# Adding the squares of the feed-forward norms on VectorE instead of GpSimd in a two-layer decoder trunk

## What is computed

```python
def rms_norm(x, g):
    xf = x.astype(jnp.float32)
    y = xf * lax.rsqrt(jnp.mean(xf * xf, axis=-1, keepdims=True) + EPS)
    return y.astype(x.dtype) * g

for l in range(DEPTH):                       # DEPTH = 2
    if l == 0: xp = xp + attention_a(rms_norm(xp, g_attn[0])) @ w_o_a[0]
    else:
        k, v = rms_norm(xp, g_kv) @ w_kv_s   # shared keys and values
        xp = xp + attention_b(rms_norm(xp, g_attn[1]), k, v) @ w_o_b[0]
    gate, up = rms_norm(xp, g_ffn[l]) @ w_gate_up[l]
    xp = xp + (silu(gate) * up) @ w_down[l]
y = rms_norm(xp, g_final)
```

## Time and profile before

| | |
|---|---|
| median of three runs | 2483.86 us (2478.34 to 2485.71) |
| the profiled execution | 2487.55 us, of which the span is 2485.8 |
| PE busy | 2366.3 us, 95% of the span |
| DVE, ACT, POOL busy | 1588.7, 812.5, 265.8 us |
| mean granted clock of PE | 0.976 of full speed |

### The profile page before, as it was taken

One profiled execution on the slowest core, in us unless ns is written; L12 is line 12 of the kernel. 1 busy time (PEld: TensorE's weight loads), 2 busy tenths in 40 slices (PEclk: granted clock), 3 DMA queues, 4 the chain that ended last, 5 costly groups with the idle time before them and its releaser, 6 DMA issues. The chain is left out here.

```text
span 2485.8 us, 43568 instructions
## 1 busy us (share of the span) xinstructions
PE 2366.3 (95%) x17709; PEld 2277.6 (92%) x17709; DVE 1588.7 (64%) x3174; ACT 812.5 (33%) x1863; POOL 265.8 (11%) x216
## 2 busy tenths in 40 slices
PE   8999899999999999998999998787999999999996
PEld 8888699999999999998999876477999999999996
DVE  6466647776766767667212377557767667676666
ACT  4344435222222222224110187544222222222224
POOL 3343200000000000004211110521000000000002
PEclk9999999999999999999999999888999999999998
DMA  4010211141313131110221233711131313131112
GB/s 179 21 54 18 90 51 40 47 150 48 114 49 113 52 110 43 52 48 21 87 70 42 83 95 135 266 51 35 52 112 50 113 49 119 44 110 52 51 35 73
DMA packets 79043, 187.93 MB, mean 76 GB/s; under 512 B 10968, under 2 KB 40024, under 8 KB 78072
## 3 DMA queue, kind: packets, MB, share of 16 engines
q1 hardware_dynamic: 77944, 180.45, 22.3%
q0 software_dynamic: 912, 4.85, 0.5%
HBM read 175.85 MB, written 44.70 MB: 89 GB/s over the span
## 5 line engine op out<-in xcount | busy, mean ns | idle before, releaser
L1532 DVE TENSOR_TENSOR XT<-XT,PS 128x768 f32<-128x768 f32 x382 | 257.9, 716 | 112.4 <-PE PS L2474 111.2
L2474 PE MATMUL PS<-HH,SLH 128*128 128x384 f32 (+1 forms) x1050 | 231.8, 329 | 8.1 <-DVE XT L1532 6.0
L2474 PE MATMUL PS<-HL,SLH 128*128 128x384 f32 (+1 forms) x1050 | 231.2, 328 | 0.0
L2474 PE MATMUL PS<-HH,SLL 128*128 128x384 f32 (+1 forms) x1050 | 231.0, 328 | 0.0
L2377 PE MATMUL PS<-TH_T,SLH 128*128 128x272 f32 x1056 | 219.0, 289 | 2.4 <-issue 2.4
L2377 PE MATMUL PS<-TL_T,SLH 128*128 128x272 f32 x1056 | 219.6, 289 | 0.0
L2377 PE MATMUL PS<-TH_T,SLL 128*128 128x272 f32 x1056 | 219.4, 289 | 0.0
L2474 PEld LDWEIGHTS PS<-HH,SLH 128*128 128x128 f32 x1050 | 177.4, 188 | 9.9 <-issue 9.9
L2474 PEld LDWEIGHTS PS<-HL,SLH 128*128 128x128 f32 x1050 | 178.1, 188 | 0.0
L2474 PEld LDWEIGHTS PS<-HH,SLL 128*128 128x128 f32 x1050 | 178.0, 188 | 0.0
L2377 PE MATMUL PS<-TH_B,SLH 128*128 128x272 f32 x792 | 166.6, 292 | 6.2 <-DVE SLL L1579 6.2
(11 more groups left out here) (323 smaller groups left out, 5303.9 us busy)
## 6 DMA issues: line engine op xcount, KB each, us to landing
ROW<-in_w_gu SPq DMA_DIRECT2D x88, 512.0 KB, 3.6
ROW<-in_w_dn SPq DMA_DIRECT2D x44, 512.0 KB, 4.0
out_bkS<-in_bk_in SPq DMA_DIRECT2D x8, 2032.0 KB
out_bvS<-in_bv_in SPq DMA_DIRECT2D x8, 2032.0 KB
KC<-in_bk_in SPq DMA_DIRECT2D x8, 1536.0 KB, 10.5
VC<-in_bv_in SPq DMA_DIRECT2D x8, 1536.0 KB, 7.0
XT<-in_xT SPq DMA_DIRECT2D x16, 544.0 KB, 5.4
RAW<-in_w_qB SPq DMA_DIRECT2D x12, 512.0 KB, 3.6
```

The source lines that it names most:

```text
L1532: ins = nc.vector.tensor_tensor(x, x, ps, ALU.add)
L2474: ins = mm(PS[:, 3 * j + i, 0:width], w[:, k * P:(k + 1) * P], x[:, a:a + width], start=(k == 0 and n == 0), stop=(k == 1 and n == 2))
```

## The change

It has three parts. All squares of norms 2, 3 and 4 are added on DVE, and POOL adds none. For norms 2 and 4, the squares of the eight tiles get a place each (tile 0's is the total itself), so ACT does not wait for adds and tile 0 needs none; norm 2's adds stand together behind the loop, norm 4's stand in it. In the second output projection, ACT squares a tile after the operands and not ahead of them, DVE adds the square of the tile before, `T1`'s low parts come one tile later and `T2`'s after tile 5, with the piece lists changed to match.

```diff
 PIECES_LO = (
...
-    ["B110", "B111", "B112", "B210", "T10", "T20", "T30", "B211", "T11", "T21", "T31", "B212", "T12", "T32", "T22", "D6",
-     "D7", "B220", "B221", "B222", "T42", "T40", "T41"])
+    ["B110", "B111", "B112", "B210", "T30", "B211", "T31", "T10", "B212", "T32", "T11", "D6", "T20", "T21", "D7", "T22", "T12",
+     "B220", "B221", "B222", "T42", "T40", "T41"])
...
-        SQ2, SQS2 = at("SQ2", [P, 2, TOK], R), at("SQS2", [P, MT * P], R + 2 * W4)
-        SQ_OF, SQS_OF = (SQ, SQ1, SQ2, SQ1, SQ2), (SQS, SQS1, SQS2, SQS1, SQS2)
+        SQS2 = at("SQS2", [P, MT * P], R)
+        SQ2 = [SQS2] + [at(f"SQ2{k}", [P, TOK], R + 4 * P * MT + W4 * (k - 1)) for k in range(1, KT)]
+        SQS_OF = (SQS, SQS1, SQS2, SQS1, SQS2)
+
+        def square_home(norm, k, j):
+            return (SQ2[k][:, 0:TOK] if norm in (2, 4) else (SQ, SQ1)[norm % 2 if norm < 2 else 1][:, j, :])
...
             scale("kB", 2, 0, 1)
-            for k in range(KT):
-                add_squares(2, k)
+            pool.wait_ge(S["sq"], 2 * KT + 1)
+            nc.gpsimd.memset(SQS2[:, TOK:], 0.0).then_inc(S["pad"], 1)
             scale("kB", 2, 1)
...
-            for k in range(KT - 1):
-                add_squares(3, k)
-            for k in range(KT - 2):
-                add_squares(4, k)
...
                 q = KT * norm + k
-                if q >= 2:
+                if norm in (0, 1, 3) and k >= 2:
                     act.wait_ge(S["sqs"], q - 1)
...
                     act.wait_ge(S[f"free{j}"], PLAN.groups[name] + m // 2 + 1)
                     if m == KT - 1:
                         direct_hi(l, 7)
-                    squares(norm, m, j)
                     if l == 0:
+                        squares(norm, m, j)
                         operands_first(m)
                     else:
                         operands_second(m)
+                        squares(norm, m, j)
...
             def last_square(c):
                 a, w = CH[c]
                 act.wait_ge(S["tres"], c + 1)
-                act.wait_ge(S["sqs"], 5 * KT - 2)
...
             def add_squares(norm, k, j):
 
                 dve.wait_ge(S["sq"], KT * norm + k + 1)
-                if isinstance(k, int) and k == 0:
+                if norm in (2, 4) and k == 0:
+                    dve.sem_inc(S["sqs"], 1)
+                elif k == 0:
...
-                if m in (3, 4):
+                if m in (3, 4, 5):
                     kk = m - HP
                     block_lo(1, "B21", kk)
                     sum_of(1, "T2", kk)
                     sum_of(1, "T4", kk)
                     sum_of(1, "T3", kk)
-                    sum_lo(1, "T1", kk)
-                    sum_lo(1, "T2", kk)
                     sum_lo(1, "T3", kk)
...
+                    if kk:
+                        sum_lo(1, "T1", kk - 1)
                 if m == 6:
                     prepare(1, 0)
                     prepare(1, 1)
                     direct_lo(1, 6)
+                    sum_lo(1, "T2", 0)
+                    sum_lo(1, "T2", 1)
+                    add_squares(3, 6, 0)
                 if m == 7:
                     prepare(1, 2)
                     direct_lo(1, 7)
+                    sum_lo(1, "T2", 2)
+                    sum_lo(1, "T1", 2)
...
                     add_tile(m, j).then_inc(S[f"free{j}"], 1)
-                    if l == 0 and 0 < m < KT - 1:
+                    if 0 < m < KT - 1:
                         add_squares(norm, m - 1, (m - 1) % 2)
...
                     if final and l == 0 and m > 1:
                         low(2, m - 2)
+                    if final and l == 1 and m > 1:
+                        add_squares(4, m - 2, 0)
...
                     split_lo(PLAN.first["kB"] + 1, 1, KT)
+                    for k in range(KT):
+                        add_squares(2, k, 0)
```

More of the change, by code:

```diff
@@ L815, in squares @@
                 q = KT * norm + k
-                if q >= 2:
+                if norm in (0, 1, 3) and k >= 2:
                     act.wait_ge(S["sqs"], q - 1)
-                nc.scalar.activation(SQ_OF[norm][:, j, :], XT[:, ds(k * TOK, TOK)], ACT.Square).then_inc(S["sq"], 1)
+                nc.scalar.activation(square_home(norm, k, j), XT[:, ds(k * TOK, TOK)], ACT.Square).then_inc(S["sq"], 1)
             def high(k):
@@ L1048, in operands_second @@
                     sum_hi(1, "T3", kk)
[L1049 to L1052, removed]
                 if m == 6:
@@ L1298, in last_square @@
                 act.wait_ge(S["tres"], c + 1)
-                act.wait_ge(S["sqs"], 5 * KT - 2)
-                nc.scalar.activation(SQ2[:, 1, a:a + w], XT[:, (KT - 1) * TOK + a:(KT - 1) * TOK + a + w],
+                nc.scalar.activation(SQ2[KT - 1][:, a:a + w], XT[:, (KT - 1) * TOK + a:(KT - 1) * TOK + a + w],
                                      ACT.Square).then_inc(S["tsq"], 1)
@@ L1358, in add_squares @@
                 dve.wait_ge(S["sq"], KT * norm + k + 1)
-                if isinstance(k, int) and k == 0:
-                    nc.vector.tensor_copy(SQS_OF[norm][:, 0:TOK], SQ_OF[norm][:, 0, :]).then_inc(S["sqs"], 1)
+                if norm in (2, 4) and k == 0:
+                    dve.sem_inc(S["sqs"], 1)
+                elif k == 0:
+                    nc.vector.tensor_copy(SQS_OF[norm][:, 0:TOK], square_home(norm, 0, 0)).then_inc(S["sqs"], 1)
                 else:
@@ L1363, in add_squares @@
                     total = SQS_OF[norm][:, 0:TOK]
-                    nc.vector.tensor_tensor(total, total, SQ_OF[norm][:, j, :], ALU.add).then_inc(S["sqs"], 1)
+                    nc.vector.tensor_tensor(total, total, square_home(norm, k, j), ALU.add).then_inc(S["sqs"], 1)
             def rstd(norm, columns=False):
@@ L1645, in operands_second @@
                     sum_of(1, "T3", kk)
-                    sum_lo(1, "T1", kk)
-                    sum_lo(1, "T2", kk)
                     sum_lo(1, "T3", kk)
-                if m == 5:
-                    block_lo(1, "B21", 2)
-                    sum_of(1, "T2", 2)
-                    sum_of(1, "T4", 2)
-                    sum_of(1, "T3", 2)
-                    sum_lo(1, "T1", 2)
-                    sum_lo(1, "T3", 2)
-                    sum_lo(1, "T2", 2)
+                    if kk:
+                        sum_lo(1, "T1", kk - 1)
                 if m == 6:
@@ L2039, in last_sum @@
                 dve.wait_ge(S["tsq"], c + 1)
-                nc.vector.tensor_tensor(SQS2[:, a:a + w], SQS2[:, a:a + w], SQ2[:, 1, a:a + w], ALU.add).then_inc(S["tadd"], 1)
+                nc.vector.tensor_tensor(SQS2[:, a:a + w], SQS2[:, a:a + w], SQ2[KT - 1][:, a:a + w], ALU.add).then_inc(S["tadd"], 1)
             def last_reciprocal(c):
```

## The result

The changed kernel takes 2469.34 us, median of 6 runs (2465.31 to 2473.39), and the kernel before 2484.78 beside it (6 runs, 2478.34 to 2487.12): ratio 0.9942, 95% interval 0.9926 to 0.9957. The gain is 15.4 us of medians; 8.5 were forecast. The forecast of the time itself was 2475.4 us, with a range of 2469 to 2482, so the measured median lies inside the range by only 0.3 us. The profiled executions, 2487.55 and 2468.99 us, lie 18.6 apart. 2.5 us of that is there before the first changed instruction: layer 0's last row of residual adds starts at 1130.24 before and 1127.72 after. So I compare distances within a stretch, not times since the start.

A forecast was written before the change was run, and what follows sets the result against it. DVE instructions with two SBUF operands were taken to stand still while POOL adds, making PE wait. Terms -8.1 + 1.2 - 1.6 = -8.5 took the profiled 2487.55 to 2479.0 us, less 3.7 for the median: 2475.4, range 2469 to 2482.

The forecast's parts named there:

- What bounds the kernel: At the three places where POOL adds squares, DVE instructions with two SBUF operands stand still meanwhile, and PE waits for DVE.
- Rival C: Slower, 2490 us: stretched DVE instructions are not freed when POOL stops, `TL_B` keeps 2.49 us; chance 0.05.
- rival A: Smaller gain, 2478.3 us: semaphore waits break the overlap of DVE steps, -5.6 instead of -8.5; chance 0.35.
- Rival B: Larger gain, 2471.9 us: PE keeps full clock at norm 2's sums, -2.3 there instead of +1.2, -12.0 in all; chance 0.17.
- Layer 1's output projection: Second output projection: steps between adds fall from 10.3 to 8.3 us, add 7 comes 8.5 sooner; part worth -8.1 us.
- Behind add 7: Second product after a long PE idle: half clock costs about 2.1 us, all but 0.4 hidden by the column sums' 1.68.
- After layer 0: kB and norm 2's sums: sums start 2.6 us earlier but at half clock, kB tile 1 starts at 1180.4; +1.2 us.
- After layer 1: End of layer 1: DVE's slices and residual adds no longer held up, `last_sum(0)` starts at 2464.6 instead of 2466.21; -1.6 us.
- The sum: Whole kernel: -8.1 + 1.2 - 1.6 = -8.5 us on the profiled execution; 2475.4 us forecast for the median.

The follow-up runs named there:

- old_order: Changed kernel with the second output projection's operands, squares and pieces in the order of before, all adds still on DVE; 2468.38 us.
- tail: Changed kernel with two low parts of T2 and the add of tile 6's square moved behind the residual add of tile 7, second output projection; 2465.26 us.
- n2_pool: Changed kernel with norm 2's adds (end of layer 0) given back to POOL, squares keeping their eight places; 2471.08 us.
- n4_pool: Changed kernel with norm 4's first six adds (end of layer 1) given back to POOL; 2470.95 us.
- interleave: Changed kernel with norm 2's adds spread over DVE's waits instead of seven in a row, the second kB split behind them; 2460.16 us.
- n3_pool: Changed kernel with norm 3's seven adds (layer 1's output projection) given back to POOL, new order kept; 2474.7 us.
- warm: Changed kernel with useless matmuls in PE's idle stretches: 8 before norm 2's sums, 6 behind layer 1's first product; 2469.8 us.
- spread_tail: Changed kernel with the edits of interleave and tail together; 2459.18 us.

## Why the prediction was right, and where its terms were off

**What bounds the kernel**: right. POOL's adds hold DVE up, whatever the data (POOL's idle adds gave back 6.6 of 15.4 us). Rival C, the slower case, fell with `TL_B` at 0.78 us, and rival A, the smaller gain, with distances as forecast (below). Rival B lay nearest in time (2471.9 us), though what it stood on, full clock at norm 2's sums, did not happen. That the median of 2469.3 us fell inside the range is in part luck: two stretches came out 3.6 and 3.2 us better than forecast, and the range's lower end had been set for the runs' scatter.

**Layer 1's output projection**, up to add 7: right within 0.3 us at each add. Ends of adds 2 to 7 gained 1.0, 2.4, 4.4, 6.4, 8.8 and 8.8 against 1.0, 2.25, 4.2, 6.2, 8.65 and 8.5 forecast, counted from the add of tile 0; distances 8.3, 8.3, 7.44 and 8.92 against 8.3, 8.3, 7.4 and 9.0. But I read the two parts of this change as one. The runs part them: the adds' move is worth 7.2 to 8.6 us, the new order 1.6 with POOL's adds and 0.2 without. Of the 2.42 + 1.28 us that I priced between adds 6 and 7, the two adds belong to the first part and the low parts to the new order, whose last distance is 0.8 longer than that of `old_order`. `tail`, which moves the low parts and one add behind add 7, took 2.5 off.

**Behind add 7**: mis-sized. I put -0.4 for half clock on the next products, to be hidden at the column sums. The half clock came (0.66 us a pair), and PE ran late enough that it no longer waited for the gate, as forecast. But the column sums then took 2.05 instead of 3.31 us, and the products after them ran at full clock instead of at half for four microseconds. 2.8 us were gained, not lost. Four executions with the same instructions from there on took 35.15 (the changed kernel), 36.74, 37.06 and 36.70 us (`n2_pool`, `n4_pool`, `interleave`) against 37.99 in the one execution of before; the other eight profiled executions lie between 35.1 and 37.2. An estimate from these four is that 1.2 us or so belong to the change and the other 1.6 to this execution; with one profile of before, the split stays open.

**After layer 0**: the times were right, the clock was not. kB's first split came 6.9 us sooner (6.7 forecast) and the sums 2.6 sooner (2.6 forecast), both against the residual add. But kB tile 0, which I left at the 14.6 us of the earlier trace rows, took 12.1: it had half clock before behind 3.52 us in which PE stood idle, and I took that idle time away without taking its price away. That by itself gained no time, since the sums had to wait for the seven adds anyway; it only made PE's wait 6.63 us long. What set the result came behind it. From start to start, the sums took 3.8 us at half clock where I had 4.6, the column sums 2.0 where I had 3.3, and the first 15 matmuls of kB tile 1, at full clock now, 2.6 where they had taken 4.1 before. These 0.8, 1.3 and 1.5 are the 3.6 us between +1.2 and -2.4. The result is near rival B's -2.3, though by another way than B's. `n2_pool` gives the same 2.4 back.

**After layer 1**: -2.0 against -1.6, given back in full by `n4_pool` (2.0).

**The sum.** With what the runs confirm, the terms are 2.4, 8.8, 1.2 to 2.8 and 2.0: 14.4 to 16.0, around the 15.4 of the medians. The forecast named the mechanism and DVE's and ACT's part of it (8.5 of 8.8, 1.6 of 2.0); the step that failed is the PE clock, counted as a cost of new idle time at the second product, at the sums and at the column sums, and never as a gain where the kernel before had run at half clock (kB tile 0 and tile 1, and layer 1's column sums and the products behind them). The profiled execution of before lay 2.8 above the median of six runs, where I had set 3.7.

## What to carry to other kernels

Before work goes to POOL because it is idle, look at the DVE instructions beside it: where one of them lies on a chain, an add on POOL (2.5 us) can hold that chain up by most of its own length (1.9 us for the split of `n3_pool`), and the same add on DVE costs it 1.2 to 1.4 us at most. When a wait of PE goes away, reprice the matmuls behind it too, since they may have been at half clock because of it. And of a reordering, ask for the last instruction before each release: here three that nobody needed yet stood ahead of the add that PE waited for.

## What the runs showed of the hardware

- A DVE instruction with two SBUF operands that was issued while POOL added ended behind POOL by nearly the whole time that it takes alone: by 0.28 us for 256 elements (`n4_pool`; alone 0.42), 0.56 for 512 (`n3_pool`; alone 0.69), 0.57 for 544 (alone 0.78) and 1.08 for 1024 (alone 1.22; second split of kB in the changed kernel: 1158.79, POOL's product 1154.73 with 2.98 us). Between two POOL instructions in a row it was let in. Neither a DVE instruction that had started before POOL's nor an add to x, with one operand in PSUM, was held. In the kernel before, the first low part started ahead of POOL's three adds and took 1.28 us, and the add to x inside them 1.34, no more than elsewhere:

```profile
1134.41 1.28 DVE L1353 TENSOR_TENSOR XL<-XT,XH 128x1088 fp32r<-128x1088 f32 x1
1135.13 10.06 POOL L693 TENSOR_TENSOR SQS<-SQS,SQ 128x1088 f32<-128x1088 f32 x3 [1.15 <-ACT SQ L818]
1139.19 1.34 DVE L1532 TENSOR_TENSOR XT<-XT,PS 128x768 f32<-128x768 f32 x2
```

- It goes both ways: the product just named took 2.98 us, the next one 1.95; the longer one was issued while DVE was at a low part (1154.66, 1.29 us).
- The same length of idle time did not give the same clock behind it. In the kernel before, PE went on at 0.74 us per three matmuls behind 2.99 us of idle time, and at 1.09 behind 2.10. At the last tile of layer 0, with the same list, the changed kernel went on at 1.01 behind 1.88 us and `warm` at 0.74 behind 1.87.
- The granted clock can fall to half with PE never idle, behind the 18 one-column matmuls of the column sums, and the same instructions behave differently from one execution to the next. `interleave` went on at 1.25 us per three matmuls, `spread_tail`, with the same list there, at 0.74:

```profile
1163.86 2.17 PE L2116 MATMUL PS<-ONES,SQS 128*128 128x1 f32 x18
1165.89 0.74 PE L2079 MATMUL PS<-XH,WH 128*128 128x384 f32 x3
```

- With the added fp32 matmuls of `warm` in PE's idle stretch the granted clock was 1.00 there, where the changed kernel had 0.59. Whether the fall behind the column sums comes from the one-column matmuls was not tried.
